# A two-block transformer kernel: the memory-attention chain with its sums, rstd, turned copies and renewals in another order, and half 0's squares summed by TensorE

## The reference, cut to what matters

```python
def second_block(x, mem, ...):
    ...
    x = x + rms_norm(merged @ w_mix_out[l], mix_post_g[l])
    h = rms_norm(x, xa_pre_g[l])
    mem_n = rms_norm(mem, mem_g[l])
    x = x + rms_norm(mem_attention(h, mem_n, w_xq[l], w_xkv[l], w_xo[l]), xa_post_g[l])
    h = rms_norm(x, ffn_pre_g[l])
    x = x + rms_norm(conv_ffn(h, w_up[l], ...), ffn_post_g[l])

def mem_attention(h, mem_n, w_xq, w_xkv, w_xo):      # 4 heads of 128, 256 memory rows
    q = (h @ w_xq).reshape(B, S, X_HEADS, X_HEAD_DIM)
    ...
    s = jnp.einsum("bqhd,bmhd->bhqm", q, k) / math.sqrt(X_HEAD_DIM)
    p = jax.nn.softmax(s, axis=-1)
    o = jnp.einsum("bhqm,bmhd->bqhd", p, v).reshape(B, S, X_W)
    return o @ w_xo
```

## Time and profile before

| | us |
|---|---|
| median of 3 runs | 2921.78 |
| lowest and highest | 2920.51, 2922.21 |
| the profiled execution, its time | 2927.9 |
| its span | 2926.0 |
| mean granted clock of TensorE | 0.984 |

### The profile page before, as it was taken

How to read it: one execution, slowest core, us unless ns; L and a number is a source line. 1 busy time by engine, 2 the same in 40 slices (tenths; PEclk the granted TensorE clock), 3 DMA queues, 4 the chain that set the end, 5 groups by cost and what they waited for, 6 DMA issues and landing times.

```text
span 2926.0 us, 35159 instructions
## 1 busy us (share of the span) xinstructions
PE 2823.0 (96%) x13916; PEld 2307.3 (79%) x13916; DVE 1270.6 (43%) x1788; ACT 795.1 (27%) x1234; POOL 970.0 (33%) x1008
## 2 busy tenths in 40 slices
PE   7999988999999999999999998999979999999998
PEld 6889876888888888878797776777658888888886
DVE  4266636543323223255204343458476343433436
ACT  5254426220001101143113333334452111111114
POOL 3622310743333333324332110364125333333330
PEclk9999999999999999999999999999989999999999
DMA  5423331311111111116543232432012111111103
GB/s 206 157 100 101 101 123 40 119 52 63 43 46 54 43 43 57 35 23 134 131 94 91 80 108 85 169 115 87 29 72 72 56 45 43 43 43 43 66 20 115
DMA packets 156934, 230.59 MB, mean 79 GB/s; under 512 B 5285, under 2 KB 116240, under 8 KB 156824
## 3 DMA queue, kind: packets, MB, share of 16 engines
q1 hardware_dynamic: 110448, 136.85, 16.2%
q10 hardware_dynamic: 46375, 92.24, 9.0%
HBM read 181.33 MB, written 47.74 MB: 78 GB/s over the span
## 4 chain that ended last, share of the span: by engine, by line
PE 84%; DVE 9%; ACT 3%; issue 2%; DMA 1%; ACTq 0%; POOL 0%; DVEq 0%; POOLq 0%
PE PS L906 30%; PE PS L297 22%; PE PS L919 10%; PE PS L1263 4%; PE PS L2313 3%; PE PS L1269 2%; PE PS L933 2%; PE PS L1320 2%; PE PS L1958 2%; PE PS L2028 1%; PE PS L2000 1%; PE PS L2016 1%; DVE SC L661 1%; DVE XT L1089 1%; DVE SC L1051 1%
## 5 line engine op out<-in xcount | busy, mean ns | idle before, releaser
L2942 POOL CAST wh<-raw 128x512 fp32r<-128x512 f32 (+1 forms) x488 | 336.6, 704 | 1870.4 <-issue 1185.8
L2946 POOL TENSOR_TENSOR wl<-raw,wh 128x512 fp32r<-128x512 f32 (+1 forms) x488 | 659.5, 1363 | 1.3 <-issue 1.3
L297 PE MATMUL PS<-UH,wh 128*128 128x512 f32 x1040 | 426.4, 410 | 10.6 <-DVE UL L2739 3.0
L297 PE MATMUL PS<-UH,wl 128*128 128x512 f32 x1040 | 407.9, 392 | 0.0
L297 PE MATMUL PS<-UL,wh 128*128 128x512 f32 x1040 | 407.7, 392 | 0.0
L906 PE MATMUL PS<-UL,wh 128*128 128x512 f32 x1280 | 394.1, 389 | 0.0
L906 PE MATMUL PS<-UH,wl 128*128 128x512 f32 x1280 | 394.0, 389 | 0.0
L906 PE MATMUL PS<-UH,wh 128*128 128x512 f32 x1280 | 393.9, 389 | 0.0
L906 PEld LDWEIGHTS PS<-UH,wl 128*128 128x128 f32 x1280 | 240.2, 188 | 50.0
L906 PEld LDWEIGHTS PS<-UL,wh 128*128 128x128 f32 x1280 | 240.2, 188 | 49.9
L906 PEld LDWEIGHTS PS<-UH,wh 128*128 128x128 f32 x1280 | 240.2, 188 | 49.8
(11 more groups left out here) (341 smaller groups left out, 3995.2 us busy)
## 6 DMA issues: line engine op xcount, KB each, us to landing
raw<-in_w_up SPq DMA_DIRECT2D x33, 1024.0 KB, 7.2
raw<-in_w_in SPq DMA_DIRECT2D x27, 1024.0 KB, 10.7
raw<-in_w_down SPq DMA_DIRECT2D x22, 1024.0 KB, 4.9
raw<-in_w_gate SPq DMA_DIRECT2D x11, 1024.0 KB, 5.3
raw<-in_w_out SPq DMA_DIRECT2D x8, 1024.0 KB, 6.1
xres<-XT ACTq DMA_DIRECT2D x4, 2048.0 KB, 7.3
zgate<-SC ACTq DMA_DIRECT2D x32, 256.0 KB, 2.0
SC<-zgate ACTq DMA_DIRECT2D x16, 512.0 KB, 4.4
```

What stands on the lines that cost most here:

```text
L297: mm = pe.matmul(PS[:, banks[f], :], w[:, k, f * P:(f + 1) * P], u[:, k, half(h)], start=(k == 0 and j == 0), stop=(k == n_k - 1 and j == 2))
L2942: pool.tensor_copy(wh[slot][:, cols], raw[slot % 2][:, cols]).then_inc(hi_done[slot], 1)
L2946: low = pool.tensor_tensor(wl[slot][:, cols], raw[slot % 2][:, cols], wh[slot][:, cols].bitcast(F32), ALU.subtract)
```

## The change

It reorders the programs of TensorE, ScalarE and VectorE in `Chain` and moves one sum:

- TensorE: the add-up of half 1 of `mixed` phase 0 moves from query tile 0 (k = 5) to query tile 1 (k = 3); that of phase 1 from the end of unit 4 to unit 5, ahead of turn(4). At units 16 and 18 the tiles KT+2 and KT+3 take part in pieces (two, then one k step), so four tiles are one k step short of done after the units instead of three.
- The squares of half 0 in phase 1 of `joined` are summed by TensorE, eight `total` passes between the last out tiles, instead of by VectorE and one `add_up`. The renewals of half 0 have `sums=False`. Squares that TensorE sums use three buffers instead of two.
- ScalarE: `mixed` has rstd(0,1) and then rstd(1,0), instead of both logarithms and then both roots. turned(0) moves from unit 3 to unit 2. Ln of joined(0,0) comes behind the probabilities of unit 14 and Exp before those of unit 15. Ln of joined(1,0) stands between high(6) and high(7), Exp behind.
- VectorE: the renewals 0 and 1 of half 1 move in front of the unit loop, turned(0) to unit 2, query(1,0) ahead of low(1) at unit 6, and the renewals of `joined` half 0 start at unit 15.

```diff
-                self.on_tensor, self.totals = on_tensor, counter("pooling_full", (KT - 1) * len(on_tensor))
+                self.on_tensor, self.totals = on_tensor, [counter(name, (KT - 1) * (len(on_tensor) > 0)) for name in ("pooling_full", "pooling_hi")]
...
-                    self.total(pe, 2 * k)
-                    self.total(pe, 2 * k + 1)
-
-            def total(self, pe, k):
-
-                pe.wait_ge(*self.sq[1](KT + k + 1))
-                mm = pe.matmul(PS[:, self.banks[1][1], :], ones[:], self.buf(k % 2, 1), start=k == 0, stop=k == KT - 1)
-                mm.then_inc(self.sums[1].sem if k == KT - 1 else self.totals.sem, 1)
+                    self.total(pe, 1, (2 * k, 2 * k + 1))
+
+            def total(self, pe, h, ks):
+
+                for k in ks:
+                    pe.wait_ge(*self.sq[h](KT + k + 1))
+                    mm = pe.matmul(PS[:, self.banks[h][1], :], ones[:], self.buf(k % 3, h), start=k == 0, stop=k == KT - 1)
+                    mm.then_inc(self.sums[h].sem if k == KT - 1 else self.totals[h].sem, 1)
 
             def square(self, act, h, p, k, src):
-                if k >= 2:
-                    act.wait_ge(*(self.totals(k - 1) if (h, p) in self.on_tensor else self.acc[h](p * (KT - 1) + max(1, k - 2))))
-                act.activation(self.buf(k % 2, h), src, ACT.Square).then_inc(self.sq[h].sem, 1)
+                alone = (h, p) in self.on_tensor
+                if k >= 2 + alone:
+                    act.wait_ge(*(self.totals[h](k - 2) if alone else self.acc[h](p * (KT - 1) + max(1, k - 2))))
+                act.activation(self.buf(k % (2 + alone), h), src, ACT.Square).then_inc(self.sq[h].sem, 1)
...
@@ query_tile
                     if (n, k) == (0, 5):
                         norm.add_up(pe, 0, 1)
+                    if (n, k) == (1, 3):
                         norm.add_up(pe, 1, 0)
@@ out_tile
-                    if t < 3:
+                    if t < 4:
                         pe.wait_ge(*self.o_lo(4 * h + k + 1))
@@ between
                 elif s == 16:
-                    for n in range(2):
+                    for n in (2, 3):
+                        self.out_tile(pe, KT + n, range(2))
+                    for n in (0, 1):
                         self.out_tile(pe, KT + n, (2,))
                 elif s == 18:
-                    self.out_tile(pe, KT + 2, range(3))
+                    for n in (2, 3):
+                        self.out_tile(pe, KT + n, (2,))
@@ tensor
                     self.between(pe, s)
+                    if s == 5:
+                        self.mixed.add_up(pe, 1, 1)
...
-                    if s == 4:
-                        self.mixed.add_up(pe, 1, 1)
-                for t in range(3):
-                    self.out_tile(pe, KT + t, (3,))
-                for t in range(3, KT):
-                    self.out_tile(pe, KT + t)
-                    if t == 4:
-                        self.joined.add_up(pe, 0, 1)
+                self.joined.total(pe, 0, (0, 1))
+                for t in range(KT):
+                    self.out_tile(pe, KT + t, (3,) if t < 4 else range(4))
+                    self.joined.total(pe, 0, {1: (2,), 3: (3,), 4: (4, 5, 6, 7)}.get(t, ()))
@@ scalar
-                for step in (norm.logarithm, norm.root):
-                    step(act, 0, 1)
-                    step(act, 1, 0)
+                norm.rstd(act, 0, 1)
+                norm.rstd(act, 1, 0)
...
-                    if 3 <= s < 17 and s % 2 == 1:
+                    if 5 <= s < 17 and s % 2 == 1:
                         turned((s - 3) // 2)
+                    if s == 15:
+                        joined.root(act, 0, 0)
...
-                    if s == 15:
-                        joined.rstd(act, 0, 0)
+                    if s == 2:
+                        turned(0)
+                    if s == 14:
+                        joined.logarithm(act, 0, 0)
...
-                joined.rstd(act, 1, 0)
-                joined.high(act, 0, (6, 7))
+                joined.high(act, 0, (6,))
+                joined.logarithm(act, 1, 0)
+                joined.high(act, 0, (7,))
+                joined.root(act, 1, 0)
@@ vector
                 query(0, 0)
+                dve.wait_ge(*self.res[1](32))
+                renew_second((0, 1))
                 for s in range(19):
-                    if 3 <= s < 17 and s % 2 == 1:
+                    if 5 <= s < 17 and s % 2 == 1:
                         turned((s - 3) // 2)
+                    if s == 6:
+                        query(1, 0)
+                    if s == 16:
+                        joined.renew(dve, 0, (1,), sums=False)
...
                     if s == 0:
-                        dve.wait_ge(*self.res[1](32))
-                        renew_second((0, 1))
                         divide(s)
...
                         if s == 2:
-                            norm.low_weighted(dve, 1, (6, 7))
+                            turned(0)
+                        if s == 15:
+                            joined.renew(dve, 0, (0,), sums=False)
                         if s in (2, 3, 4):
                             divide(s)
+                        if s == 2:
+                            norm.low_weighted(dve, 1, (6, 7))
...
-                        for j in {6: (0, 1), 9: (2,)}.get(s, ()):
+                        for j in {6: (1,), 9: (2,)}.get(s, ()):
                             query(1, j)
...
-                    for k in {16: (0, 1), 17: (2,), 18: (3, 4, 5)}.get(s, ()):
-                        joined.renew(dve, 0, (k,))
+                    for k in {16: (2,), 17: (3, 4), 18: (5, 6)}.get(s, ()):
+                        joined.renew(dve, 0, (k,), sums=False)
 
                 joined.accumulate(dve, 1, 0, 1)
-                joined.renew(dve, 0, (6, 7))
+                joined.renew(dve, 0, (7,), sums=False)
...
-                          store=True, on_tensor=((1, 1),))
+                          store=True, on_tensor=((0, 1), (1, 1)))
```

## The result

The changed kernel takes 2908.48 us (median of five runs, 2905.11 to 2908.91) against 2921.78 (five runs, 2920.51 to 2931.27). Over all these runs the ratio is 0.9943, 95% interval 0.9931 to 0.9955, so 16.7 us less (13 to 20); the two medians alone differ by 13.3. Two further comparisons of the same pair gave 2906.95 against 2924.31 (0.9939, 0.992 to 0.9957) and 2903.2 against 2921.71 (0.9934, 0.9918 to 0.9951). The forecast, 18.0 less, is a ratio of 0.9938 and lies inside all three intervals; the time forecast, 2903.8 (2897 to 2913), holds the time measured.

The account below looks back on a forecast made before the run. TensorE was taken as the bound, busy 96%, so only its gaps and lower clock could be won. Gains along the way, 4.15 at first scores to 17.5 to 19.1 at the last total, gave 18.0: 2921.78 to 2903.8 us (2897 to 2913).

Parts of the forecast that it names:

- The front: Start of the chain up to unit 8: first scores 4.15 us earlier, third maximum 3.4, unit 8 about 7.
- the bounds for unit 8: Gain at unit 8, taken as 7 us: 3.4 from VectorE's lead at unit 2, 8.4 from query(1,0)'s lead.
- Units 14 to 18: Ln and Exp of joined(0,0) move around the probabilities of units 14 and 15; turn(15) ends at 2114.9 instead of 2121.05.
- 3.01 gap: TensorE's wait behind turn(15), with 3 us lost at half clock, covered by 12 matmuls of tiles KT+2 and KT+3.
- The sums of half 0: Eight TensorE passes replace seven VectorE additions and one pass, 6.0 us more for TensorE; split starts at 2137.5, 17.2 earlier.
- The head: FFN head: renewals of half 1 start 18.2 us earlier, new gaps of 2.0 and 0.5, last total 17.5 to 19.1 earlier.
- the 2.55: TensorE gap in the FFN head, closing to a few tenths because UL 6 and 7 no longer wait for the whole rstd.
- (b): Rival: the front's 7 us do not arrive, gain 11, 2910.8 us; chance 0.14.
- (c): Rival: no half-clock stretch and no gap at half 1's first total, gain 23, 2898.8 us and less; chance 0.10.
- (d): Rival: TensorE waits for ScalarE at nearly every total and stays at half clock, about 10 slower, 2932 us; chance 0.04.
- (e): Rival: the split is bound by something else, only 4.0 us won, 2917.8, no change; chance 0.06.
- the table loads: Two added ScalarE loads at the chain's start, 1.28 us each; at the skill's 2.66, gain 15.2, 2906.6 us, chance 0.02.

Follow-up runs that it names:

- a2_front: The kernel before with only the changes up to unit 13, its tail left as before; 2915.66 us, ratio 0.9966 to the kernel before.
- b5_warm: The kernel before with passes over ones, results overwritten, put into its gaps of 3.01 and 9.99; 2922.05 us, ratio 0.999 to the kernel before.
- e1_hold: b4_lowfirst with GpSimd's cast of slot 0 held until the scores of unit 6 are written; 2907.6 us, ratio 0.9952 to the kernel before.
- c1_double: The changed kernel with each of the eight passes of half 0's sums done twice; 2910.63 us, ratio 0.996 to the kernel before.
- a4_vsum: The changed kernel with half 0's squares added by VectorE again and one add-up in tile KT+4; 2908.82 us, ratio 0.995 to the kernel before.
- a1_after: The changed kernel itself, run again in the first set; 2906.95 us against 2924.31 for the kernel before, ratio 0.9939.
- a3_tail: The changed kernel with the front of the kernel before, so only the tail changes remain; 2913.14 us, ratio 0.996 to the kernel before.
- b1_lnln: The changed kernel with the order Ln, Ln, Exp, Exp again at the chain's start; 2904.12 us, ratio 0.9928 to the kernel before.
- b4_lowfirst: The changed kernel with VectorE's remainders UL 6 and 7 put ahead of the third maximum; 2911.62 us, ratio 0.9955 to the kernel before.
- e0_after: The changed kernel itself, run again in the third set; 2903.2 us against 2921.71 for the kernel before, ratio 0.9934.
- e3_front_hold: The same kernel as b1_lnln, timed again in the third set, holding nothing back; 2906.07 us, ratio 0.9943 to the kernel before.
- e2_best: e1_hold with rstd(1,1) ahead of unit 5's probabilities and half 1's totals one k later; 2910.83 us, ratio 0.9958 to the kernel before.

## Why the prediction was right

The waypoints, each as the difference of before and after, less the 0.4 us by which after's first add-up starts earlier:

| place | forecast | measured |
|---|---|---|
| first scores (2015.95 to 2011.45) | 4.15 | 4.1 |
| scores of unit 8 (2068.83 to 2061.17) | 7, 3.4 to 8.4 | 7.3 |
| turn(15) ends (2121.05 to 2114.29) | 6.1 | 6.4 |
| split of half 0 (2154.70 to 2136.59) | 17.2 | 17.7 |
| renewals of half 1 (2174.12 to 2154.76) | 18.2 | 19.0 |
| last total ends (2189.28 to 2169.29) | 17.5 to 19.1 | 19.6 |

**The front.** TensorE was to be done with tile 1 at 2011.8: 2011.45. ScalarE's order costs what was summed: Exp of half 1 ends at 2011.9 (forecast 2012.3), the first maximum is at 2013.91 (2014.3), the third at 2031.66 (2032.1), 0.4 early throughout like the first add-up itself; VectorE is the limit up to unit 3 and wins the 3.4 of the forecast. Of the bounds for unit 8 the value in the middle came: query(1,0) at 2054.45 (forecast 2054.4, so 0.5 late against the shifted start), a gap of 1.16 there (1.0) and one of 0.76 behind it (1 to 2). The waits for UL 6 and 7 were put at some 5 us; they are 1.45 and 2.21, 3.7 together. a2_front has the same 7.2 at unit 8 without the tail.

**Units 14 to 18.** The 3.01 gap is covered by the products of tiles KT+2 and KT+3, as forecast; there is no gap between 2114.29 and 2142, and the clock stays at 1.00 in 2118 to 2122 and 2130 to 2134. That this lower clock had a price on the path, "3 us lost", was right in the prediction and wrong in my later expectation for b5_warm. The prediction's reading "after gaps of 2.3 us and more TensorE runs some us at 0.50" holds for the six such gaps of before, but not for every execution: it stayed at 1.00 behind 3.31 in e1_hold and behind 2.57 in a2_front.

**The sums of half 0.** "7 x 0.86 = 6.0 us more for TensorE": c1_double measures 0.87 each, all on the path. ScalarE was to write square 6 at 2130.2 and square 7 at 2132.8: they end at 2129.5 and 2132.06; total 7 ends at 2133.9 (2134.7), the split starts at 2136.59 (2137.5). The step is 0.9 early, of which 0.4 is the shift of the whole section; accumulate(1,0,1) began at 2126.58, 0.7 before the forecast of 2127.3. What the text left unsaid is how little the passes themselves bring: a4_vsum puts 3.9 of the 17.7 down to them. They cost 6.9 (less the 0.87 of the pass that goes) and save VectorE's additions beside the cast; the rest of the order, which needs no passes, brings more.

**The head.** The products wait 0.83 for the remainders of half 0, and 0.26 at the head's start, which before has as well (1.6 forecast), and none of the 2.55 is left (a few tenths forecast). The first totals of half 1 wait 1.70 and 0.20 (forecast 2.0 and 0.5), and the clock did not fall behind them (granted 1.00 in all windows from 2152 to 2162), so the last total is above the upper end of the forecast, by 0.5. In a1_after and e1_hold the same two gaps, 1.70 and 0.20, were followed by windows at 0.50, and the stretch from the split to the last total is 1.6 to 1.8 us longer for it, as the prediction had put it (1.65). In six others with a gap of 1.65 to 1.71 there (a3_tail, b1_lnln, b4_lowfirst, c1_double, e0_after, e3_front_hold) the clock stayed at 1.00; whether it falls after such a wait is not settled by its length.

**The one step that failed** is the last, the one from the profile to the median: the profile was to be 2909.9 and, because before's profile lay 6.1 above its median, the median 2903.8. The profile came as forecast within 1.4 us (2908.49), but it lies at after's median (2908.48), not 6 above it. The difference of profile and median is no constant of a kernel: over the 14 profiles it runs from -4.8 to +6.1 us, mostly in step with where the first add-up starts (1995 to 2008 us). That alone does not explain this pair, though, whose sections start within 0.4 us of each other; the cause is open. By the ratio the gain is 16.7 (13 to 20), by the section 19.6, by the three pairs of medians 13.3, 17.4 and 18.5: 18.0 is inside, and the 4.7 us between the forecast and the median are no more than this spread. The mechanism is borne out by the section and its waypoints; the medians alone could not have told a gain of 18 from one of 13.

**The rivals.** (b), the front does not arrive: a2_front is 8.6 shorter. (c), no half clock: it still stood at 0.50 from 2034 to 2040, and the gap at the first total stayed. (d), slower by the passes: no gap between them at all, clock 1.00. (e), the split bound by something else: it came 17.7 earlier. On the table loads the rows give 1.29 from a load to the next instruction, and two loads less left the section as it was (166.7 and 166.8 against 166.5 and 166.7). The Trainium skill (ScalarE: Activation LUTs, What ACT_TABLE_LOAD costs) has 2.66 us for a switch; no row here shows its drain of 1.38. By that figure the gain would have been 15.2, an estimate.

## What to carry to other kernels

Compare two kernels over the section that the change touches, cut at the same instructions, and add what lies around it last: here the section of the changed kernel repeats within 1.6 us, while its whole executions lie between 2901 and 2909 and those of before between 2916 and 2933. Before moving work from an engine to TensorE, try the reordering without it: 13.8 of 17.7 us needed no pass. When an engine gets ahead, ask which buffer it frees and what that starts: a remainder computed 2.5 us sooner brought the GpSimd cast 3 us forward, onto VectorE's additions, and cost 3.5.

## What the runs showed of the hardware

- A pair of VectorE's 128x512 additions with both inputs in SBUF takes 1.48 alone (after, 2046.67) and 2.76 beside GpSimd's work on weights (b4_lowfirst, 2053.80). The copy out of PSUM took 0.68 alone and beside it (b4_lowfirst, 2056.48). The Trainium skill (SBUF — State Buffer, Who interferes with whom) has it that a VectorE instruction with two SBUF inputs contends with a GpSimd instruction that reads SBUF, and one with at most one SBUF input, outside the 2-port modes, does not. The trace agrees for these two.
- A pair of divides of 128x256, which have one SBUF tensor as input, takes 0.62 alone and 1.55 to 2.29 beside GpSimd's work (after, b4_lowfirst, e1_hold).
- The same idle time can lower TensorE's clock or not. It dropped to 0.50 after gaps of 1.45 and 2.21 in a row (after, from 2034) and after 1.55 and 2.46 in e1_hold, not after 1.70 and 0.20 in after, but after the same two in a1_after and e1_hold. Behind 3.31 it stayed at 1.00 (e1_hold, 2042.74), behind 3.32 at the same instruction it fell (e2_best, 2047.68); behind 2.57 it stayed (a2_front), behind 2.55 at the same instruction it fell (before, 2173.65). Keeping it busy with 12 and 40 passes over the ones held it at 1.00.
- An fp32 pass over 128x512 takes two records and 0.86 us at 1.00; in after the four of totals 4 to 7 (2130.32, 3.59 for eight records) ran without idle time beside GpSimd's cast.
- The same wait can cost nothing or more, by its place and size: 1.41 in front of the down products left the clock at 1.00, 2.81 there (e2_best) brought it to 0.50 in the windows from 2226 to 2232.
